# Recurrent gates in 64-row stationary tiles on the banks of scores and numerators, and the second recurrence tile finished behind the scores' products

## What is computed

```python
def _rg_lru(x, h0, w_r, b_r, w_i, b_i, lam):
    xb = x.reshape(Bn, L, LRU_BLOCKS, LRU_BW)
    r = sigmoid(einsum('blnc,ncd->blnd', xb, w_r).reshape(Bn, L, D_LRU) + b_r)
    i = sigmoid(einsum('blnc,ncd->blnd', xb, w_i).reshape(Bn, L, D_LRU) + b_i)
    log_a = -LRU_C * r * softplus(-lam)
    a = exp(log_a)
    u = sqrt(-expm1(2.0 * log_a)) * (i * x)
    h[t] = a[t] * h[t-1] + u[t]
```

## Time and profile before

| | us |
|---|---|
| median of 3 runs | 1048.53 (1047.71 to 1052.13) |
| the profiled execution: time | 1052.81 |
| the profiled execution: span | 1050.7 |
| PE busy (matmuls) | 972.4, 93% of the span |
| DVE busy | 674.0, 64% |
| ACT busy | 547.8, 52% |
| POOL busy | 288.1, 27% |
| mean granted TensorE clock | 0.969 |

### The profile page before, as it was taken

The page is one execution under the profiler, slowest core; times in us unless marked ns, Lnnn a source line. Parts: engine busy times, 40 slices in busy tenths (PEclk is TensorE's granted clock), DMA queues, the critical chain, the costliest instruction groups (busy, mean ns, idle before and its releaser), DMA issues.

```text
span 1050.7 us, 16726 instructions
## 1 busy us (share of the span) xinstructions
PE 972.4 (93%) x5963; PEld 856.7 (82%) x5963; DVE 674.0 (64%) x865; ACT 547.8 (52%) x610; POOL 288.1 (27%) x189
## 2 busy tenths in 40 slices
PE   5999899999999998899999999949779999999984
PEld 3999789889978986799999987737668888888873
DVE  5495659767865974622111114389598989898975
ACT  5645525825542572323333323457388787878752
POOL 1013214312421441533443443005400101011161
PEclk9999999999999999899999999969989999999998
DMA  9552222303222220233233269139899999999986
GB/s 294 172 169 70 53 57 60 105 20 91 79 59 58 58 76 4 61 86 95 80 85 94 80 206 310 61 135 315 330 356 396 413 413 414 412 412 413 384 205 171
DMA packets 146951, 193.20 MB, mean 184 GB/s; under 512 B 14936, under 2 KB 92158, under 8 KB 146788
## 3 DMA queue, kind: packets, MB, share of 16 engines
q1 hardware_dynamic: 139434, 166.34, 46.0%
q0 software_dynamic: 5008, 16.23, 5.2%
q10 hardware_dynamic: 2474, 10.18, 2.5%
HBM read 172.93 MB, written 19.79 MB: 183 GB/s over the span
## 4 chain that ended last, share of the span: by engine, by line
PE 43%; POOL 4%; DVE 3%; DMA 3%; issue 3%; SPq 2%; ACT 1%; ACTq 0%; DVEq 0%; POOLq 0%
PE PJ L463 40%; POOL slot_weights L788 2%; POOL MEM L806 2%; PE MS L1509 1%; SPq L609 1%; DMA MEM<-expert_rows,MEM 1%; PE NM L1457 1%; DMA MEM<-slot_weights 1%; PE NM L1542 1%; DMA RAW<-in_w_out_dram 0%; DMA MEM<-t_rows,MEM 0%; DVE MEM L2215 0%; POOL MEM_R L684 0%; DVE MEM_R L1988 0%; PE MS L1448 0%
## 5 line engine op out<-in xcount | busy, mean ns | idle before, releaser
L463 PE MATMUL PJ<-MEM_R 128*128 128x272 f32 (+2 forms) x5016 | 807.1, 322 | 11.6 <-DVE MEM_R L2109 3.4
L463 PEld LDWEIGHTS PJ<-MEM_R 128*128 128x128 f32 x5016 | 726.0, 192 | 75.7 <-issue 10.0
L684 POOL TENSOR_TENSOR MEM_R<-RAW,MEM_R 128x1024 fp32r<-128x1024 f32 x72 | 178.8, 2492 | 319.6 <-ACT MEM_R L831 319.6
L1988 DVE TENSOR_TENSOR MEM_R<-CHUNK,MEM_R 128x2048 fp32r<-128x2048 f32 x100 | 224.5, 2285 | 26.2 <-ACT MEM_R L1089 26.0
L1089 ACT CAST MEM_R<-CHUNK 128x2048 fp32r<-128x2048 f32 x100 | 189.3, 1912 | 12.5 <-PE PJ L463 8.0
L831 ACT CAST MEM_R<-RAW 128x1024 fp32r<-128x1024 f32 x81 | 84.3, 1048 | 130.4 <-DMA RAW<-in_w_pb_dram 42.9
L1901 DVE TENSOR_TENSOR MERGED<-PJ,MEM 128x544 f32<-128x544 f32 x16 | 11.6, 725 | 143.4 <-PE PJ L463 132.3
L767 POOL COPY MEM<-MEM 128x1 uint32 (+1 forms) x16 | 19.6, 1222 | 223.2 <-PE MS L1509 223.2
L1731 DVE SCALAR_TENSOR_TENSOR MEM<-MEM 128x548 f32<-128x548 f32 x72 | 58.9, 818 | 8.5 <-DVE MEM L1729 0.9
L1098 ACT CAST MEM_R<-MS 128x1024 fp32r<-128x1024 f32 x17 | 17.3, 1018 | 33.2 <-PE MS L1509 33.2
L888 ACT COPY MEM<-PJ 128x272 f32<-128x272 f32 x24 | 9.0, 376 | 45.8 <-PE PJ L463 45.8
(11 more groups left out here) (324 smaller groups left out, 947.2 us busy)
## 6 DMA issues: line engine op xcount, KB each, us to landing
CHUNK<-in_w_gate_dram SPq DMA_DIRECT2D x34, 1024.0 KB, 7.1
CHUNK<-in_w_up_dram SPq DMA_DIRECT2D x34, 1024.0 KB, 8.8
CHUNK<-in_w_down_dram SPq DMA_DIRECT2D x34, 1024.0 KB, 8.0
RAW<-in_w_in_dram SPq DMA_DIRECT2D x56, 512.0 KB, 3.7
expert_rows<-MEM ACTq DMA_DIRECT2D x15, 512.0 KB, 6.0
expert_rows<-MEM SPq DMA_DIRECT2D x10, 512.0 KB
RAW<-in_w_pa_dram SPq DMA_DIRECT2D x8, 512.0 KB, 3.6
RAW<-in_w_pb_dram SPq DMA_DIRECT2D x8, 512.0 KB, 3.6
```

Source lines behind the costliest of these rows:

```text
L463: ins = pe.matmul(out, w(a), x(b), start=first and n == 0, stop=last and n == 2)
L684: tt(lo, raw[slot], hi.bitcast(F32), ALU.subtract).then_inc(lo_done, 1)
L1988: tt(moe_hl[c][1], moe_raw[c], moe_hl[c][0].bitcast(F32), ALU.subtract).then_inc(chunk_lo[c], 1)
```

## The change

`bd` keeps no zeros. It holds one 128-column matrix per tile: rows 0 to 63 hold the r block in columns 0 to 63 and the i block in columns 64 to 127, rows 64 to 127 hold i in columns 0 to 63 and r in 64 to 127. A product with rows 0 to 63 goes to `NM`, one with rows 64 to 127 to `MS`, in turn for each half of the columns. So each bank holds r and i of 64 channels, and ACT reads four pieces of 64 partitions where it read two of 128. The gates no longer use `PJ`: its uses are renumbered, project 8 and project 9 follow `values` directly, and `scores` waits until ACT has read all gates. On DVE `lru(hd, c)` ends after i times x; the root's product and the scans are `lru_scan`, called directly for tile 0, and for tile 1 between the five products and the `kw` tiles of `probabilities`.

```diff
-    PJ_A0, PJ_B0, PJ_LOOP, PJ_HEAD = 2, 6, 16, 14
-    PART_B = (4, 5, 6, 7, 10, 11)
+    PJ_A0, PJ_B0, PJ_LOOP, PJ_HEAD = 2, 6, 12, 10
+    PART_B = (4, 5, 6, 7, 8, 9)
...
                     for half in range(2):
-                        side = slice(64 * half, 64 * half + 64)
-                        sp.dma_start(bd[side, :, m, side], blocks[ds(hd, 1), half].rearrange("a p c d -> p (a c) d"))\
+                        side, cols = (slice(64 * s, 64 * s + 64) for s in (half, m ^ half))
+                        sp.dma_start(bd[side, :, cols], blocks[ds(hd, 1), half].rearrange("a p c d -> p (a c) d"))\
                             .then_inc(bd_in, 16)
...
-                        await_step(sp, pj_full, hd * PJ_HEAD + (PJ_B0 - PJ_HEAD + 10))
+                        await_step(sp, gates_full, hd * 2 * CT)
                         load_gates(hd)
...
-            const(pool.memset(bd, 0.0))
...
                 def gates(c):
-                    for m, name in enumerate(("br", "bi")):
-                        bank(part_b(hd) + 4 + 4 * c + m)
-                        emptied(act.activation(ri[c][:, m, :].rearrange("p (a n) -> p a n", a=2), pj(m)[:, :, 0:LN_ // 2], ACT.Sigmoid,
-                                               bias=v2t[:, ds(hd * CT + (V2C[name] + c), 1)]))
+                    sides = slice(0, 64), slice(64, P)
+                    for n, name in enumerate(("br", "bi")):
+                        for m, b in enumerate((NM, MS)):
+                            act.wait_ge(gates_full, hd * 2 * CT + (2 * c + m + 1))
+                            act.activation(ri[c][sides[m], n, :].rearrange("p (a n) -> p a n", a=2), b[sides[m ^ n], :, 0:LN_ // 2],
+                                           ACT.Sigmoid, bias=v2t[sides[m], ds(hd * CT + (V2C[name] + c), 1)]).then_inc(gates_read, 1)
...
                 for c in range(CT):
                     pe.wait_ge(conv_done, hd * 6 + (2 + 5 + c))
-                    for m in range(2):
-                        pe.wait_ge(pj_free, part_b(hd) + (4 + 4 * c + m + 1))
-                        b = pj(m)
-                        for half in range(2):
-                            last = pe.matmul(b[:, half, 0:LN_ // 2], bd[:, c, m, :], xc[:, c, half * (LN_ // 2):(half + 1) * (LN_ // 2)],
-                                             start=True, stop=True)
-                        last.then_inc(pj_full, 1)
+                    if c:
+                        pe.wait_ge(gates_read, hd * 4 * CT + 4 * c)
+                    else:
+                        pe.wait_ge(nm_free, hd + 1)
+                        pe.wait_ge(ms_free, hd * MS_HEAD + (MS_PRE + 2))
+                    for half in range(2):
+                        for b, side in ((NM, slice(0, 64)), (MS, slice(64, P))):
+                            last = pe.matmul(b[:, half, 0:LN_ // 2], bd[side, c, :],
+                                             xc[side, c, half * (LN_ // 2):(half + 1) * (LN_ // 2)], start=True, stop=True)
+                            if half:
+                                last.then_inc(gates_full, 1)
...
                 pe.wait_ge(c0_in, hd * 32 + 32)
+                pe.wait_ge(gates_read, hd * 4 * CT + 4 * CT)
                 b = ms_use(0, hd)
...
-                st.link(tt(u, u, xc[:, c, :], ALU.mult))
+                st.do(tt(u, u, xc[:, c, :], ALU.mult))
+
+            def lru_scan(hd, c):
+                u = ri[c][:, 1, :]
+                st.wait()
                 dve.wait_ge(root_ready, hd * CT + (c + 1))
                 st.link(tt(u, u, tmp[:, 3, :], ALU.mult))
...
                 lru(hd, 0)
+                lru_scan(hd, 0)
                 lru(hd, 1)
...
                     emptied(tt(d, b[0:d.shape[0], 0:d.shape[1]], d, ALU.mult))
+                lru_scan(hd, 1)
+                st.wait()
+                dve.wait_ge(lru_done, hd * CT + CT)
                 for j in range(J):
                     n = rows_of[j]
                     b = misc(hd, 6 + j // 2)
```

More of the change, by code:

```diff
@@ L214, in hawk_mlstm_hmoe_kernel @@
         v1, v2, v1t, v2t = at("v1", P), at("v2", P), at("v1t", P), at("v2t", P)
-        bd = at("bd", CT, 2, P)
+        bd = at("bd", CT, P)
         gcol = at("cols", J, 2 * H)
@@ L366, in hawk_mlstm_hmoe_kernel @@
         nm_full, nm_free = sem("nm_full"), sem("nm_free")
+        gates_full, gates_read = sem("gates_full"), sem("gates_read")
         steps_v, steps_a, steps_p = sem("steps_v"), sem("steps_a"), sem("steps_p")
@@ L404, in hawk_mlstm_hmoe_kernel @@
         CONSTS, LATE_CONSTS = [0], [0]
-        NCONST, NLATE = 12, 13
+        NCONST, NLATE = 11, 13
         ORDER = [JP] + list(range(JP))
@@ L939, in gates @@
                 def gates(c):
-                    for m, name in enumerate(("br", "bi")):
-                        bank(part_b(hd) + 4 + 4 * c + m)
-                        emptied(act.activation(ri[c][:, m, :].rearrange("p (a n) -> p a n", a=2), pj(m)[:, :, 0:LN_ // 2], ACT.Sigmoid,
-                                               bias=v2t[:, ds(hd * CT + (V2C[name] + c), 1)]))
+                    sides = slice(0, 64), slice(64, P)
[4 more added lines that the diff above has]
+                                           ACT.Sigmoid, bias=v2t[sides[m], ds(hd * CT + (V2C[name] + c), 1)]).then_inc(gates_read, 1)
                 def decay(c):
-                    act.wait_ge(pj_free, part_b(hd) + (2 + 4 + 4 * c + 1))
+                    act.wait_ge(gates_read, hd * 4 * CT + (4 * c + 2))
                     if c:
@@ L963, in second_part @@
                     high_group(hd, 11 + m)
-                    bank(part_b(hd) + 6 + m)
+                    bank(part_b(hd) + 4 + m)
                     emptied(act.activation(og[:, m, :].rearrange("p (a n) -> p a n", a=2), pj(m)[:, :, 0:HB], ACT.Sigmoid))
```

## The result

The changed kernel takes 1062.26 us in the median of 6 runs (1061.39 to 1063.98), against 1048.18 for the kernel before; the ratio is 1.0126, 95% interval 1.0106 to 1.0147: 11 to 15 us slower. The profiled execution took 1062.29 with a span of 1060.3.

The account below looks back on a forecast made before the run. PE, busy 93% of the span, was taken as the bound. First turn 1.7 + 1.5, two loop turns 2.3 + 1.5 each, last turn -1.8: +9.0 on the median 1048.5 gives 1057.5 us, range 1045 to 1064.

Parts of the forecast that it names:

- last turn: Stretch from gates to project 1 behind the loop: scans run alone, `dsum` ready 1.8 us earlier, -1.8 at 402.32.
- The gates on PE: Eight gate records per group on PE: 1.4 us instead of 2.11, gain 0.7 per group, bounds 1.06 and 2.11.
- ACT: ACT's four gate pieces, priced 0.72 for the last and 0.66 start to start; tile 1's last ends 0.4 us later.
- A turn in the loop: From tile 0's gates to project 1: scans collide with POOL's subtractions, project 1 starts 2.3 us later, bounds 0.1 and 2.9.
- the copy's wait: Sign of being right: PE's wait for the old state's copy, 0.34 us before, shrinks to nothing.
- The clock: After PE idles over 4 us before project 1, the granted clock falls: 1.5 us lost per turn, bounds 0 and 2.0.
- third rival: Head rounds: no collision, and the clock's slow stretches go too: -9.0 us, 1039.5; chance 0.12.
- The first turn: Head 0, tile 0's gates to project 1: project 1 starts at 123.7 for 121.97, +1.7 us, and the clock takes 1.5.
- 1, clock holds: Turns: DVE's scans collide with POOL, but PE's clock does not drop: +4.5 us, 1053.0; chance 0.16.
- 2, no collision: Turns: POOL's pieces end before the five products, or the port lock does not bite: -3.1 us, 1045.4; chance 0.16.
- 4, no overlap: PE's gates: 64-row products do not overlap, turns end up to 1 us later each: +12, 1060.5; chance 0.10.

Follow-up runs that it names:

- tiles only: The changed kernel with the second tile's root product and scans back at the end of the round, 64-row gates and new banks kept: 1056.89 and 1056.98 us.

## Why the prediction was right, and where its size was off

The direction, the place and the mechanism were right: 1062.3 lies in the range of 1045 to 1064. The size was low: +9.0 forecast, +14.1 between the medians with an interval of 11 to 15, which leaves +9.0 out. Profile against profile the change is +9.5 (1062.29 for 1052.81), almost the +9.0 of the sum, but that is luck: as the steps below show, a clock loss that was priced too low and a slow projection that went, which the forecast did not have, cancel each other. Luck has a part in the range too. Its upper end adds 1.5 for the last turn, where the step itself takes 1.8 away, and the prediction gives no reason; with the step's own -1.8 the upper end is 1060.2, below what was measured.

The steps, against the first profile of each:

**The gates on PE.** Taken 1.4 a group, gain 0.7; measured 1.13 to the next projection for 2.19, gain 1.06, near the end of the bounds with all in pairs. The two records of a pair start 0.00 to 0.04 apart. The Trainium skill's rule (TensorE: Matmul & The Clock Gate, on packing small matmuls) was the better guide than counting records of one product in a row. If changing the rows costs something, it is little: the whole group with its ends takes 1.13 where eight records in pairs would take 1.06.

**ACT.** Four pieces of 0.71, 0.74 from start to start (0.72 and 0.66 taken): a piece of 64 partitions takes as long as one of 128 with as many columns. The predicted end of tile 1's pieces was 0.4 later against the gates of tile 0; measured 17.64 for 17.27, 0.4. Not foreseen: ACT then waits 0.24 more before `decay`, for tile 0's scan, which comes later by the same pieces.

**A turn in the loop.** +2.3 taken, **+2.6** measured (33.24 for 30.62), with the root's product and the scan where the step put them: they end 28.27 and 31.55 behind the gates for the step's 28.2 and 31.6, and the scan ends 1.08 behind POOL's end for 1.09. The rule of the skill (SBUF — State Buffer, two separate sides), an exclusive lock for the whole instruction, agrees with these rows and with the run in which POOL waits, where the scan's 3.11 became 1.22. One of the signs that the prediction named did not come: the copy's wait did not shrink to nothing but was 0.42 for 0.34, because PE's lead had grown to about what the copy gained. A part left out of the sum was the 0.3 us between scan and `kw`, a wait that DVE has for its own result.

**The clock.** This is the term that was mis-sized: 1.5 a turn was taken, 2.1 to 2.3 measured (8.38, 8.47, 8.55 for 6.30). Against it, the projection behind the tiny matmuls ran at full clock in each round (6.26 for 7.8), which the prediction had only in its third rival: -1.5 a round. Together the round grew by 3.35 (gates to gates 95.44 for 92.09), where 3.8 was taken. The two sizes nearly cancel. (The row that the prediction calls five score products, 4.73 for 3.34, has 16 records, which are the last four; its loss of 1.4 stays.)

**The first turn.** +1.7 and 1.5 taken. Measured: 2.3 and 2.1, less the 1.5; 2.9 together, 3.2 with a start 0.3 later.

**The last turn.** -1.8 taken, -2.2 measured at the numerators (32.47 for 34.68 us behind the gates). **This is the step that failed, though not in its own number: it ends at 402 and carries the gain on from there, with nothing for the clock behind it.** What came next was the clock again. PE's timeline of the changed kernel there:

```profile
407.56 0.39 PE L1312 MATMUL MS<-MEM 128*32 128x128 f32 x2 [2.18 <-DVE MEM L1795]
410.06 0.77 PE L1319 MATMUL MS<-MEM 128*128 128x128 f32 x2 [2.11 <-DVE MEM L1800]
...
411.90 6.50 PE L1324 MATMUL NM<-MEM 128*128 128x512 f32 x16
...
435.81 0.70 PE L1349 MATMUL MS<-MEM 128*128 128x256 f32 x2 [2.13 <-DVE MEM L1830]
...
437.58 8.83 PE L464 MATMUL PJ<-MEM_R 128*128 128x272 f32 x48
```

PE now waits 2.18 for `kw` and then 2.11 for `dsum`, with little between, and the numerators' 16 records take 6.50 for 5.83 (granted clock 0.50 from 410 to 416). Then comes the wait of 2.13 and a projection of 8.83. At the mark only 1.0 of the 2.2 is left against the first profile of before; against the second, with the short form, the stretch is 3.0 **slower** (83.73 for 80.70). The prediction took the one profile, 4.3 above the median, as an execution like the others and moved its difference over to the median. It was the long form, and the profile that lies at the median (1048.28) has the short one. So far as that one profile speaks for the median, this is 4 of the 5 us that were missing.

The sum then, second profile of before to the first of the changed kernel: start 0.6, three rounds 2.8 + 3.3 + 3.4, last stretch 3.0, rest 1.1: 14.2, which is the difference of the spans.

**The rivals.** 1, clock holds: fell in the profile, and filling the wait gave back 2.1 to 2.3 a turn where it had priced 1.5. 2, no collision: fell. The run with POOL waiting is its world, at 1051.7 rather than 1045.4: from gates to gates its first round is 1.3 longer than in the second profile of before and the next two 0.2 each, since the clock still fell behind waits of 2.6, and its stretch behind the loop is 3.0 longer, in the long form. 3, slow stretches go: half right. The slow projections did go, but beside the collision. Without it, they went in the version with the scans behind the sums, which is below this rival's 1039.5. 4, no overlap: fell.

## What to carry to other kernels

Work moved off one wait lands ahead of another: list what the next reader of that engine waits for, and give the moved step a place where the engine idles (here behind the sums, where DVE idled for 7 us), even if it takes a region of its own. Before an operation with two SBUF inputs is moved on DVE, look what POOL does in the new place. And a profile that lies off its kernel's median may be another form of the same program: ask which stretch makes it so before its difference is moved over.

## What was not expected of the hardware

- More work on PE made the kernel faster: 3.6 us of unused products in a wait saved 2.2 us of each following projection, since the granted clock stayed at 1.00, which is 2.4 GHz.
- PE arriving earlier at a wait that ends no earlier can cost: with tiles only, a wait grown from 1.47 to 4.85 us went with the last four score products taking 5.28 for 3.25. It need not: behind a wait of 2.83 the same row took 3.34 in one profile and 5.84 in the other.
- One program has forms that differ by 4.2 us at the mark, by where the low clock falls behind the loop: in a projection ahead of a wait it costs 1.5 and shortens the wait, behind it it costs 2.0 and more.
